# Expert stage: the token vectors of the U dot products are read from PSUM in place of SBUF

## The chip, the cores and the metric

The kernel runs on one core of one Trainium2 chip. The metric is the device time of one execution in microseconds (us). Five engines work side by side, each with its own stream of instructions: TensorE (PE in the profile), VectorE (DVE), ScalarE (ACT), GpSimd (POOL) and SyncE (SP), which only issues transfers here. They wait for one another through semaphores.

## The reference, cut to what matters

Two transformer blocks on 256 tokens of 1024 numbers. The first ends in a layer that retrieves single-neuron experts. That layer is the one that the change touches: `h` is the normed activation, every token picks 16 experts of 16384 in each of 8 heads, so 128 rows of `expert_u` and 128 rows of `expert_v` for each token.

```python
def peer_ffn(h, w_query, sub_keys, expert_u, expert_v):
    q = jnp.einsum('bsd,dk->bsk', h, w_query).reshape(B, S, PEER_HEADS, 2, PEER_HALF)
    sc = jnp.einsum('bshpc,hpnc->bshpn', q, sub_keys)
    s1, i1 = lax.top_k(sc[..., 0, :], 16)
    s2, i2 = lax.top_k(sc[..., 1, :], 16)
    cand_s, cand_i = (16 x 16 sums of s1 and s2), (i1 * 128 + i2)
    top_s, sel = lax.top_k(cand_s, 16)
    idx, gates = cand_i[sel], softmax(top_s)
    # for each chunk of 128 tokens (c), 8 heads (h), 16 experts (k):
    u = expert_u[idx]                                     # (c, h, k, 1024)
    a = gelu(einsum('cd,chkd->chk', h, u)) * gates
    return einsum('chk,chkd->cd', a, expert_v[idx])
```

The first block then adds this to its residual, and the second block (four gated feed-forward layers, an RWKV mixer, a differential attention) follows.

## The kernel before, in words

Up to the expert stage the kernel computes the first block's modulation, projections, attention and the second norm. The normed activation lies feature-major in `hf` (128 partitions of features, 256 tokens in the free dimension), split into two fp32r parts `hh` and `hl` for matmuls.

**Front of the expert stage.** For the first four heads (`EARLY_HEADS`) PE projects the queries (`project`), ACT copies them out of PSUM (`query_out`, L1643), PE multiplies them with the keys (`key_scores`, L1577, banks 2 and 3 in turn) and ACT copies the scores to SBUF (`key_scores_out`, L1649). Beside the first two heads PE also turns `hf` to token-major (`turn_h2`, L1566: eight 128x128 transposes for each half of the tokens, into banks 4 and 5 for tokens 0 to 127 and 6 and 7 for tokens 128 to 255), and ACT copies these banks to `h2tok` in SBUF (`h2_out`, L1636, four copies of 128x512; `h2tok` is a piece of the buffer `aux`). DVE ranks: `rank_experts(u)` finds, for one of the 16 units (two token halves times eight heads), the 16 experts of each of 128 tokens, with max, max-index, replace and 128x256 tensor operations (L1735 to L1787). It writes 16 columns of `expert`, the row numbers.

**The loop.** `STEPS` is 268 steps, one for each of the 256 rows (`NROW`) and `LAG` = 12 more. Row r is one expert for each of 128 tokens: partition p holds the 1024 numbers of the expert of token p. In step i

- POOL issues an indirect DMA that gathers U row i, and one that gathers V row i - 12 (`gather`, L1706). Each moves 128 x 4 KB = 512 KB from HBM. They go to a ring of 12 places (`ring_rows`: 8 in `big`, 2 in `hf`, 2 in `aux`), and POOL waits in `slot_free` until the last user of the place is through with it. The row numbers are read from `expert`, in SBUF.
- DVE waits for U row i to land and forms the 128 dot products (`dot_product`, L1798): a scalar_tensor_tensor over 128x1024 fp32, in0 the row, in1 the tokens' vectors `h2tok[:, r // P, :]`, with a sum to one column of `dots`. Then it does three instructions of the ranking of a unit two ahead, and every eighth step the coefficients (L1809).
- ACT computes gelu of eight dots every eighth step (L1685) and writes diag(coefficient) 128x128 for each V row (L1692), some two steps ahead of its use.
- PE multiplies diag by the V row, two fp32 matmuls of 128x512 (L1616), and accumulates tokens 0 to 127 in banks 4 and 5, and tokens 128 to 255 in banks 6 and 7. Four of the last rows are added by DVE (L1818, L1821).

Heads 4 to 7 have their query projections and key scores inside the first 64 steps, in pieces on PE; `lo.upto` and `hi.upto` (L320 on DVE, L316 on ACT) split weights into high and low parts, a few of them in these steps. Units 0 to 7 rank the first half of the tokens, units 8 to 15 the second. At step 144 DVE adds the first half's result (`add_experts(0)`, L1836 and L1838), and at step 160 POOL issues two small operations (`final_rstd(0)`, L1712 and L1715).

The order on every engine is that of the code; nothing is planned by costs.

Of the kernel before, what the change touches and what calls it, by code (L numbers as in the profile page):

```python
# [17 lines left out]
F32 = mybir.dt.float32  # L18
# [3 lines left out]
ALU = mybir.AluOpType  # L22
# [3 lines left out]
P = 128  # L26
D = 1024
# [60 lines left out]
def build_program(nc, A, out):  # L88
    ctx = ExitStack()
    with ctx:  # L90
# [33 lines left out]
        w_f = sb("w_f", [P, KT, HEADS])  # L124
        bank = [ctx.enter_context(nc.psum_tensor(f"bank{i}", [P, 512], F32)) for i in range(8)]

# [33 lines left out]
        gt1, gt2 = aux[:, 0:D], aux[:, D:2 * D]  # L160
        h2tok = aux[:, 2 * D:4 * D].rearrange("p (a d) -> p a d", a=TT)

# [1394 lines left out]
        def peer_pe(pe):  # L1557
# [3 lines left out]
            def turn_h2(tt):  # L1561
                pe.wait_ge(S("norm_hf"), 8)
                for half in range(2):
                    for j in range(4):
                        k = 4 * half + j
                        mm = pe.transpose(bank[4 + 2 * tt + half][:, j * P:(j + 1) * P],  # L1566
                                          hf[:, k, tt * P:(tt + 1) * P], ident[:, :])
                    mm.then_inc(S("h2tok_tr"), 1)
# [12 lines left out]
            for h in range(EARLY_HEADS):  # L1581
# [3 lines left out]
                key_scores(h)  # L1585
            pe.wait_ge(S("h2tok"), 4)

# [42 lines left out]
        def peer_act(act, hi):  # L1630
            norm_act(act, 1, hi)

            def h2_out(tt):
                for half in range(2):
                    act.wait_ge(S("h2tok_tr"), 2 * tt + half + 1)
                    act.activation(h2tok[:, tt, half * 512:(half + 1) * 512], bank[4 + 2 * tt + half][:, :], ACT.Copy)\  # L1636
                       .then_inc(S("h2tok"), 1)

# [24 lines left out]
            for h in range(EARLY_HEADS):  # L1663
                hi.upto(QRY + h + 2)
                query_out(h)
                key_scores_out(h)
                if h < 2:
                    h2_out(h)
            for i in range(STEPS):
# [6 lines left out]
                if at == 12 and unit < PEER_HEADS - EARLY_HEADS:  # L1676
                    key_scores_out(unit + EARLY_HEADS)
                if i in (0, 13):
                    gate_exp(min(i, 1))
# [111 lines left out]
        def peer_dve(dve, lo, o):  # L1791
            norm_dve(dve, 1, None)

            def dot_product(r):
                turn = u_turn(r)
                row = ring_rows[turn % RROWS]
                row_landed(dve, turn)
                dve.scalar_tensor_tensor(out=row, in0=row, scalar=1.0, in1=h2tok[:, r // P, :], op0=ALU.mult, op1=ALU.mult,  # L1798
                                         accum_out=dots[:, r:r + 1]).then_inc(S("u_used"), 1)
# [67 lines left out]
            lo.upto(QRY + 4)  # L1867
            dve.wait_ge(S("h2tok"), 4)
            ranking = rank_experts(dve, o, 1)
# [1431 lines left out]
```

## Time and profile before

| | |
|---|---|
| median of 3 runs | 2146.63 us |
| lowest and highest | 2139.64 and 2147.71 us |
| the profiled execution's own time | 2155.59 us |
| its span | 2153.8 us |
| granted TensorE clock, mean | 0.977 of full speed |
| busy | PE 1916.3, DVE 1321.4, ACT 806.7, POOL 641.9 us |
| bytes moved by the POOL queue (software_dynamic) | 270.83 MB |
| the gathers (L1706) | first issued at 267.8 us, last at 963.6 us of the span |

The profile is of one execution. Its span is cut in 40 slices for an overview of busy shares; the chain of work that ended last is followed back from the end; groups of instructions are listed with their busy time and the idle time before them. Windows of the trace give the same for a stretch, with the busy share of the 16 DMA engines and the rate that they moved. A row of the timeline has the start in us, the duration in us, engine, line, operation, the written and read names, and in brackets how long the engine sat idle before it and what ended that.

### The profile page before, as it was taken

To read this page: it belongs to the slowest core of one execution; us is meant where nothing else is said; L and a number is where in the kernel's file an instruction comes from. 1 tells how busy PE (TensorE), PEld (TensorE's weight loads), DVE (VectorE), ACT (ScalarE), POOL (GpSimd) and SP (SyncE) were. 2 spreads that over 40 slices of the span, in tenths; PEclk is the share of its full clock that TensorE was granted. 3 is DMA by queue.
4 is the path that set the end of the run, shared out by engine and by line. 5 is a ranking of instruction groups with operands and counts; after the bars stand their busy time and mean duration, and the time that the engine had idled before them with its cause. 6 is when DMAs were issued, how large, how long until landed. Compare 5 with 4: busy or idle time off the path is not lost.

```text
span 2153.8 us, 30579 instructions
## 1 busy us (share of the span) xinstructions
PE 1916.3 (89%) x11797; PEld 1402.5 (65%) x11797; DVE 1321.4 (61%) x2173; ACT 806.7 (37%) x1285; POOL 641.9 (30%) x644
## 2 busy tenths in 40 slices
PE   6999968877777777779999999899999999979999
PEld 4997854422222222227888888888888888868887
DVE  4777686677667656546456765465456545575544
ACT  2335432222111211114445473344443443564443
POOL 1000087777777777762000004340000000000000
PEclk8999989999999999999999999999999999979999
DMA  9982399999999999995554220055554555424553
GB/s 353 321 294 76 118 369 394 402 409 409 409 409 395 383 378 380 380 409 173 194 177 155 98 98 4 27 172 193 180 193 137 175 181 190 146 70 138 193 181 114
DMA packets 255566, 510.35 MB, mean 237 GB/s; under 512 B 14810, under 2 KB 173228, under 8 KB 252380
## 3 DMA queue, kind: packets, MB, share of 16 engines
q1 hardware_dynamic: 177898, 233.95, 32.8%
q0 software_dynamic: 74416, 270.83, 32.2%
q10 hardware_dynamic: 3138, 4.00, 0.6%
q8 instruction: 77, 1.26, 0.2%
q14 instruction: 37, 0.30, 0.0%
HBM read 507.68 MB, written 1.05 MB: 236 GB/s over the span
## 4 chain that ended last, share of the span: by engine, by line
PE 57%; POOL 17%; DMA 10%; issue 7%; DVE 6%; ACT 3%; SPq 0%; DVEq 0%; ACTq 0%
PE bank L640 22%; PE bank L668 11%; POOL big L1706 11%; PE bank L410 10%; DMA big<-in_peer_v,aux 5%; PE bank L1616 3%; POOL aux L1706 3%; POOL hf L1706 3%; DMA hf<-in_peer_v,aux 2%; DMA big<-in_w_mod 2%; PE bank L2413 1%; PE bank L370 1%; PE bank L683 1%; DVE w_lo L320 1%; ACT w_hi L316 1%
## 5 line engine op out<-in xcount | busy, mean ns | idle before, releaser
L320 DVE TENSOR_TENSOR w_lo<-w_raw,w_hi 128x2048 fp32r<-128x2048 f32 x198 | 453.6, 2293 | 271.7 <-ACT w_hi L316 271.5
L316 ACT ACTIVATE w_hi<-w_raw 128x2048 fp32r<-128x2048 f32 x198 | 378.3, 1912 | 229.6 <-PE bank L640 108.0
L1616 PE MATMUL bank<-big 128*128 128x512 f32 x676 | 338.8, 626 | 102.3 <-DMA big<-in_peer_v,aux 100.2
L1616 PEld LDWEIGHTS bank<-big 128*128 128x128 f32 x676 | 117.2, 192 | 309.9 <-DMA big<-in_peer_v,aux 221.4
L1798 DVE SCALAR_TENSOR_TENSOR big<-big,aux 128x1024 f32<-128x1024 f32 x172 | 210.5, 1225 | 148.0 <-DMA big<-in_peer_u,aux 147.7
L640 PE MATMUL bank<-w_hi,hh 128*128 128x512 f32 x704 | 278.9, 396 | 2.8 <-DVE x L1467 1.7
L640 PE MATMUL bank<-w_lo,hh 128*128 128x512 f32 x704 | 274.4, 390 | 0.0
L640 PE MATMUL bank<-w_hi,hl 128*128 128x512 f32 x704 | 265.7, 390 | 0.0
L1706 POOL DMA_INDIRECT big<-in_peer_u,aux x172 | 180.9, 1052 | 76.2 <-issue 52.1
L410 PE MATMUL bank<-hh,w_hi 128*128 128x256 f32 x672 | 194.3, 289 | 3.5 <-DVE w_lo L320 3.1
L1706 POOL DMA_INDIRECT big<-in_peer_v,aux x172 | 181.7, 1056 | 52.4 <-issue 39.0
L410 PE MATMUL bank<-hl,w_hi 128*128 128x256 f32 x672 | 192.4, 286 | 0.0
L410 PE MATMUL bank<-hh,w_lo 128*128 128x256 f32 x672 | 192.3, 286 | 0.0
L930 POOL TENSOR_TENSOR big<-big 128x512 f32<-128x512 f32 x15 | 19.9, 1325 | 474.2 <-ACT big L559 473.8
L640 PEld LDWEIGHTS bank<-w_hi,hh 128*128 128x128 f32 x704 | 132.3, 188 | 29.4 <-issue 3.5
L640 PEld LDWEIGHTS bank<-w_hi,hl 128*128 128x128 f32 x704 | 132.2, 188 | 28.2
L640 PEld LDWEIGHTS bank<-w_lo,hh 128*128 128x128 f32 x704 | 132.4, 188 | 26.2
L1685 ACT ACTIVATE aux<-aux 128x8 f32<-128x8 f32 x32 | 6.7, 208 | 370.4 <-DVE big L1798 253.4
L1692 ACT ACTIVATE big<-ident,aux 128x128 f32<-128x128 f32 x252 | 84.0, 390 | 162.5 <-DVE aux L1809 146.7
L410 PEld LDWEIGHTS bank<-hh,w_hi 128*128 128x128 f32 x672 | 131.3, 195 | 6.4 <-DVE w_lo L320 3.5
L410 PEld LDWEIGHTS bank<-hl,w_hi 128*128 128x128 f32 x672 | 131.4, 195 | 0.1
L410 PEld LDWEIGHTS bank<-hh,w_lo 128*128 128x128 f32 x672 | 131.2, 195 | 0.0
(453 smaller groups left out, 3342.7 us busy)
## 6 DMA issues: line engine op xcount, KB each, us to landing
w_raw<-in_ffn_w_in SPq DMA_DIRECT2D x176, 512.0 KB, 4.6
w_raw<-in_ffn_w_out SPq DMA_DIRECT2D x44, 1024.0 KB, 4.9
big<-in_w_mod SPq DMA_DIRECT2D x24, 1024.0 KB, 7.7
w_raw<-in_w_in SPq DMA_DIRECT2D x22, 1024.0 KB, 9.5
w_raw<-in_rwkv_w_rkv SPq DMA_DIRECT2D x12, 1024.0 KB, 5.2
w_raw<-in_peer_w_query SPq DMA_DIRECT2D x8, 1024.0 KB, 5.6
w_raw<-in_w_kv SPq DMA_DIRECT2D x8, 1024.0 KB, 5.5
w_raw<-in_w_out SPq DMA_DIRECT2D x4, 1024.0 KB, 5.1
```

Of the source, the lines that this page charges most:

```text
L316: act.activation(w_hi[i][:, :], w_raw[i][:, :], ACT.Copy).then_inc(S("w_hi"), 1)
L320: dve.tensor_tensor(w_lo[i][:, :], w_raw[i][:, :], w_hi[i][:, :].bitcast(F32), ALU.subtract)\
L370: return pe.matmul(b[:, part * CW:(part + 1) * CW], lhs, rhs, start=first, stop=last, skip_group_check=True)
L410: mm = pe.matmul(b[:, part * CW:(part + 1) * CW], lhs, rhs, start=(k == 0 and m == 0), stop=(k == KT - 1 and m == 2))
L640: return pe.matmul(bank[b + tt][:, :], a[:, k, tt * P:(tt + 1) * P], w[:, j, :], start=first and half == 0, stop=last and half == 1, skip_ ...
L668: mm = pe.matmul(bank[4 + part][:, :], ap[:, a * T + tt * P:a * T + (tt + 1) * P], wp[:, a, half * 512:(half + 1) * 512], start=(first and ...
L683: mm = pe.transpose(bank[b][:, a * T + tt * P:a * T + (tt + 1) * P], act_f[:, tt, a * P:(a + 1) * P], ident[:, :])
L1616: mm = pe.matmul(bank[4 + 2 * tt + half][:, :], diag[:, r % VDIAGS, :], ring_rows[turn % RROWS][:, half * 512:(half + 1) * 512], start=(r ...
L1692: act.activation(diag[:, r % VDIAGS, :], ident[:, :], ACT.Copy, scale=dots[:, r:r + 1])\
L1706: pool.indirect_dma_start(ring_rows[turn % RROWS], None, table, bass.IndirectOffsetOnAxis(ap=expert[:, r:r + 1], axis=0))\
L1798: dve.scalar_tensor_tensor(out=row, in0=row, scalar=1.0, in1=h2tok[:, r // P, :], op0=ALU.mult, op1=ALU.mult, accum_out=dots[:, r:r + 1]). ...
L2413: mm = pe.matmul(wkv_slot(name, g)[r, col], m[lhs][r, col], m[rhs][r, col], **alone)
```

## The change

PSUM is now declared as four pairs of banks (`bank_pair`), with `bank[i]` a half of a pair. The tokens' vectors that `dot_product` reads are the pairs themselves: pair 3 (banks 6 and 7) for tokens 0 to 127, and pair 1 (banks 2 and 3) for tokens 128 to 255.

- PE transposes the first half of the tokens into banks 6 and 7, and the second half into banks 4 and 5.
- ACT's copies out of PSUM are two in place of four: those of the first half are gone, and those of the second half go to `h2_rest` in SBUF after head 1.
- A new ACT copy, 128x1024 from `h2_rest` to banks 2 and 3 (`h2_second`), stands at step 82, after all key scores have been read.
- DVE waits for the transposes (`h2tok_tr`) before the loop, and at row 128 for `h2_second`. PE waits for the two copies to `h2_rest`.

```diff
-        bank = [ctx.enter_context(nc.psum_tensor(f"bank{i}", [P, 512], F32)) for i in range(8)]
+        bank_pair = [ctx.enter_context(nc.psum_tensor(f"bank_pair{i}", [P, 1024], F32)) for i in range(4)]
+        bank = [bank_pair[i // 2][:, i % 2 * 512:(i % 2 + 1) * 512] for i in range(8)]
...
-        h2tok = aux[:, 2 * D:4 * D].rearrange("p (a d) -> p a d", a=TT)
+        h2tok = [bank_pair[3], bank_pair[1]]
+        h2_rest = aux[:, 2 * D:3 * D]
...
-                        mm = pe.transpose(bank[4 + 2 * tt + half][:, j * P:(j + 1) * P],
+                        mm = pe.transpose(bank[6 - 2 * tt + half][:, j * P:(j + 1) * P],
...
-            pe.wait_ge(S("h2tok"), 4)
+            pe.wait_ge(S("h2_rest"), 2)
...
-            def h2_out(tt):
+            def h2_out():
                 for half in range(2):
-                    act.wait_ge(S("h2tok_tr"), 2 * tt + half + 1)
-                    act.activation(h2tok[:, tt, half * 512:(half + 1) * 512], bank[4 + 2 * tt + half][:, :], ACT.Copy)\
-                       .then_inc(S("h2tok"), 1)
+                    act.wait_ge(S("h2tok_tr"), 3 + half)
+                    act.activation(h2_rest[:, half * 512:(half + 1) * 512], bank[4 + half][:, :], ACT.Copy)\
+                       .then_inc(S("h2_rest"), 1)
+
+            def h2_second():
+                act.wait_ge(S("key_scores_read"), PEER_HEADS)
+                act.wait_ge(S("h2_rest"), 2)
+                act.activation(h2tok[1][:, :], h2_rest, ACT.Copy).then_inc(S("h2_second"), 1)
...
-                if h < 2:
-                    h2_out(h)
+                if h == 1:
+                    h2_out()
...
+                if i == 5 * TOPK + 2:
+                    h2_second()
...
-                dve.scalar_tensor_tensor(out=row, in0=row, scalar=1.0, in1=h2tok[:, r // P, :], op0=ALU.mult, op1=ALU.mult,
+                if r == P:
+                    dve.wait_ge(S("h2_second"), 1)
+                dve.scalar_tensor_tensor(out=row, in0=row, scalar=1.0, in1=h2tok[r // P][:, :], op0=ALU.mult, op1=ALU.mult,
...
-            dve.wait_ge(S("h2tok"), 4)
+            dve.wait_ge(S("h2tok_tr"), 2)
```

The order of PE, DVE, POOL and SP is the same row for row; ACT's changes in two places. First ACT before, at the front of the expert stage (L1643 and L1649 are the query and score copies, L316 a weight split, L1636 the copies of the tokens' vectors):

```order
L316 ACTIVATE w_hi<-w_raw 128x2048
L1643 ACTIVATE big<-bank 128x512
L1649 ACTIVATE big<-bank 128x2x256
L1636 ACTIVATE aux<-bank 128x512 x2
L316 ACTIVATE w_hi<-w_raw 128x2048
L1643 ACTIVATE big<-bank 128x512
L1649 ACTIVATE big<-bank 128x2x256
L1636 ACTIVATE aux<-bank 128x512 x2
L316 ACTIVATE w_hi<-w_raw 128x2048
```

The same place now, with the line numbers of the changed kernel (L318 the split, L1650 and L1656 the query and score copies, L1638 the copies to `h2_rest`):

```order
L318 ACTIVATE w_hi<-w_raw 128x2048
L1650 ACTIVATE big<-bank_pair 128x512
L1656 ACTIVATE big<-bank_pair 128x2x256
L318 ACTIVATE w_hi<-w_raw 128x2048
L1650 ACTIVATE big<-bank_pair 128x512
L1656 ACTIVATE big<-bank_pair 128x2x256
L1638 ACTIVATE aux<-bank_pair 128x512 x2
L318 ACTIVATE w_hi<-w_raw 128x2048
```

The first pair of copies is gone, so the weight split behind it moves up by two instructions. The second place, in the loop at step 82, ACT now (L1694 gelu, L1701 the diagonals, L1644 the new copy):

```order
L1694 ACTIVATE aux<-aux 128x8
L1701 ACTIVATE big<-ident,aux 128x128 x2
L1644 ACTIVATE bank_pair<-aux 128x1024
L1701 ACTIVATE big<-ident,aux 128x128 x6
L1661 ACT_TABLE_LOAD
```

The eight diagonals of one group are now parted by one copy. On DVE the rows stand as they did, with another second input; before, right behind the last instruction of the first ranking:

```order
L1787 TENSOR_TENSOR aux<-w_f 128x16
L320 TENSOR_TENSOR w_lo<-w_raw,w_hi 128x2048 x2
L1798 SCALAR_TENSOR_TENSOR big,aux<-big,aux 128x1024
L1735 MAX aux<-big 128x8 x2
L1739 MAX_INDEX aux<-aux,big 128x8
L1798 SCALAR_TENSOR_TENSOR big,aux<-big,aux 128x1024
```

And now:

```order
L1796 TENSOR_TENSOR aux<-w_f 128x16
L322 TENSOR_TENSOR w_lo<-w_raw,w_hi 128x2048 x2
L1809 SCALAR_TENSOR_TENSOR big,aux<-big,bank_pair 128x1024
L1744 MAX aux<-big 128x8 x2
L1748 MAX_INDEX aux<-aux,big 128x8
L1809 SCALAR_TENSOR_TENSOR big,aux<-big,bank_pair 128x1024
```

Nothing has moved; the dot product reads one SBUF buffer and one pair of banks in place of two SBUF buffers.

## Rows read from the trace of the kernel before

**Rows 1.** Page, chain of work that ended last, by engine and by line:

```profile
PE 57%; POOL 17%; DMA 10%; issue 7%; DVE 6%; ACT 3%; SPq 0%; DVEq 0%; ACTq 0%
PE bank L640 22%; PE bank L668 11%; POOL big L1706 11%; PE bank L410 10%; DMA big<-in_peer_v,aux 5%; PE bank L1616 3%; POOL aux L1706 3%; POOL hf L1706 3%; DMA hf<-in_peer_v,aux 2%; DMA big<-in_w_mod 2%; PE bank L2413 1%; PE bank L370 1%; PE bank L683 1%; DVE w_lo L320 1%; ACT w_hi L316 1%
```

**Rows 2.** Windows: length, busy (x) of PE, PEld, DVE, ACT, POOL; clock, DMA share, GB/s:

```profile
285.00:312.00 27.00, 12.27 (x32) 6.55 (x31) 26.38 (x67) 5.91 (x13) 22.38 (x15) 0.62 1.04 395
312.00:339.00 27.00, 21.16 (x82) 12.06 (x80) 17.63 (x38) 8.71 (x18) 21.56 (x18) 1.00 0.97 358
339.00:420.00 81.00, 69.75 (x227) 35.16 (x226) 59.21 (x144) 20.95 (x46) 63.08 (x59) 1.00 1.02 403
420.00:690.00 270.00, 208.56 (x432) 73.44 (x431) 184.22 (x471) 55.21 (x145) 206.44 (x211) 0.99 1.03 409
690.00:906.00 216.00, 153.77 (x311) 52.41 (x309) 138.49 (x349) 41.92 (x110) 168.30 (x157) 1.00 0.99 378
906.00:933.00 27.00, 22.16 (x43) 7.96 (x44) 12.47 (x21) 2.77 (x9) 20.54 (x22) 0.95 1.03 410
```

**Rows 3.** Line L1706, 420 to 690 us: ns min/median/max; time to landing:

```profile
L1706 POOL DMA_INDIRECT big<-in_peer_v,aux x70: 933/937/1096, 419.9 to 686.0; - x70
...
DMA to landing us min/median/max: 7.7/9.2/10.2
```

**Rows 4.** The same line, 690 to 906 us:

```profile
L1706 POOL DMA_INDIRECT big<-in_peer_v,aux x52: 933/1060/1912, 695.9 to 902.3; - x52
...
DMA to landing us min/median/max: 5.4/6.1/9.0
```

**Rows 5.** Timeline of POOL, 656 to 660 us: two gathers in a row:

```profile
656.77 0.93 POOL L1706 DMA_INDIRECT hf<-in_peer_v,aux  x1 [0.31 <-issue]
658.01 1.94 POOL L1706 DMA_INDIRECT aux<-in_peer_u,aux  x1 [0.30 <-issue]
```

**Rows 6.** Timeline of DVE, the same stretch:

```profile
656.60 1.28 DVE L1836 TENSOR_TENSOR big<-bank,aux 128x512 f32<-128x512 f32 x2
657.91 1.22 DVE L1838 TENSOR_TENSOR x<-x,big 128x1024 f32<-128x1024 f32 x1
```

**Rows 7.** Timeline of POOL, 705 to 712 us:

```profile
705.01 0.94 POOL L1706 DMA_INDIRECT hf<-in_peer_u,aux  x1 [0.30 <-issue]
706.25 1.37 POOL L1706 DMA_INDIRECT hf<-in_peer_v,aux  x1 [0.30 <-issue]
...
709.17 1.58 POOL L1706 DMA_INDIRECT aux<-in_peer_v,aux  x1 [0.30 <-issue]
```

**Rows 8.** Timeline of DVE, the same stretch:

```profile
704.97 0.42 DVE L1781 TENSOR_REDUCE aux<-amask 128x16 f32<-128x256 f32 x1
...
705.59 1.22 DVE L1798 SCALAR_TENSOR_TENSOR big<-big,aux 128x1024 f32<-128x1024 f32 x1
...
708.71 1.23 DVE L1798 SCALAR_TENSOR_TENSOR big<-big,aux 128x1024 f32<-128x1024 f32 x1 [0.74 <-DMA big<-in_peer_u,aux]
```

**Rows 9.** Groups of DVE instructions by line and shape, whole span:

```profile
L1798 DVE SCALAR_TENSOR_TENSOR big<-big,aux 128x1024 f32<-128x1024 f32 x172 | 210.5, 1225 | 148.0 <-DMA big<-in_peer_u,aux 147.7
...
L857 DVE SCALAR_TENSOR_TENSOR big<-bank,small,big 128x256 f32<-128x256 f32 x88 | 38.5, 480 | 87.5 <-ACT big L778 87.5
...
L1775 DVE TENSOR_TENSOR amask<-aux,small 128x256 f32<-128x256 f32 x32 | 13.6, 425 | 1.1
...
L2718 DVE SCALAR_TENSOR_TENSOR hf<-x,vec,big 128x256 f32<-128x256 f32 x8 | 3.4, 480 | 0.0
```

**Rows 10.** Timeline of POOL at the first gather:

```profile
267.79 3.11 POOL L1706 DMA_INDIRECT big<-in_peer_u,aux  x1 [24.03 <-DVE aux L1784]
```

**Rows 11.** Timeline of DVE at the first gather:

```profile
267.48 4.49 DVE L320 TENSOR_TENSOR w_lo<-w_raw,w_hi 128x2048 fp32r<-128x2048 f32 x2
```

**Rows 12.** ACT copies: L1636, and the group nearest to the new one:

```profile
L1636 ACT ACTIVATE aux<-bank x4: 593/600/606, 257.8 to 265.9; 128x512 f32<-128x512 f32 x4
...
L1660 ACT ACTIVATE hh<-x 128x1024 fp32r<-128x1024 f32 x2 | 2.1, 1049 | 13.2 <-DVE x L1838 13.2
```

## The prediction

> **What bounds the kernel now.** I start with the chain of work that ended last [rows 1]. The reader is to see that the indirect gathers stand in it as POOL instructions at L1706 in three names (11, 3 and 3%, together POOL's 17% of the 2153.8 us span) and as transfers of V rows (5 and 2% in the named groups). So while the expert stage runs, some 700 us (the first gather was issued at 267.8 us, the last at 963.6), the pace of the gathers is the pace of the kernel. Everything behind the stage waits for it and shifts with it as a whole.
>
> Next, the windows of the stage [rows 2]. Between 420 and 690 us the 16 DMA engines are busy all the time (share 1.03) and move 409 GB/s; the window at 906 shows 410. No window goes above, so I take 409 to 410 as the ceiling of the transfers. A gather is 0.524 MB, so at the ceiling one passes every 0.524 / 0.409 = 1.28 us and a step of two every 2.56 us. From 690 to 906 the rate is only 378, in 312 to 339 it is 358, in 339 to 420 it is 403, in 285 to 312 it is 395.
>
> Why the rate falls is in line L1706. In the fast stretch the V gathers' median is 937 ns and a gather lands 9.2 us after its issue [rows 3]; with 1.28 us a gather, seven are under way, so there is a queue. In the slow stretch the median of the V gathers in `big` is 1060 ns, up to 1912, and the landing takes 6.1 us, down to 5.4 [rows 4]: the queue has drained, and POOL no longer issues fast enough. Free, POOL needs 0.937 + 0.30 us (the gap before each [rows 5, 7]) = 1.24 us a gather, a little under the 1.28; it has only 0.04 us of slack.
>
> What stretches a gather is seen by laying the two timelines over each other. At 705.01 a gather starts beside a DVE reduction with one input and takes 0.94. At 706.25 one starts inside the dot product that runs from 705.59 to 706.81 and ends at 707.62, 0.81 after it. At 709.17 one starts inside the dot product of 708.71 to 709.94 and ends at 710.75, again 0.81 after it [rows 7, 8]. So a gather needs something near its start that the dot product holds until it ends. It is not DVE as such: at 656.77 a gather runs whole beside L1836, a product of a PSUM bank and an SBUF buffer, in 0.93 us, and the next, at 658.01, starts 0.10 us into L1838, a sum of two SBUF buffers that ends at 659.13, and takes 1.94, to 659.95, 0.82 behind it [rows 5, 6]. That pair is the experiment in small: two SBUF inputs hold the gather, one PSUM and one SBUF input do not.
>
> The Trainium skill, "SBUF — State Buffer", section "Who interferes with whom", says that a DVE instruction with two SBUF inputs contends with a GpSimd instruction that reads SBUF, and one with at most one SBUF input does not. The gather reads its row numbers from SBUF; the pair of rows agrees. The same section infers that a two-input tensor_tensor does not hold descriptor generation, since that writes; by that sentence this change would give nothing. The 1.94 us beside L1838 speak against it.
>
> **The change part by part.** The sum is made against the profiled execution's own 2155.59 us (span 2153.8).
>
> Removed: the hold of 256 dot products on the gathers. In 690 to 906 POOL is busy 168.30 us for 157 instructions; at 0.937 each that would be 147.1, so 21.2 us are stretch [rows 2, 4]. Of this 157 x 0.04 = 6.3 us lay in POOL's slack, and 15 remain. By bytes: 216 x (1 - 378/409) = 16.4 us. I take 16.4. In 312 to 339 it is 27 x (1 - 358/409) = 3.4 us, and there too POOL is busy 21.56 for 18 gathers, 16.9 when free, so it never waits. In 339 to 420 it is 81 x (1 - 403/409) = 1.2 us. In 285 to 312 it would be 0.9, but DVE is busy 26.38 of 27 us there and would not go faster; I count nothing. In 420 to 690 the stretch (206.44 - 211 x 0.937 = 8.7 us) lies beside a full DMA queue and brings nothing. Sum: 21.0 us.
>
> What stays held: the weight splits L320, two SBUF inputs; the first gather takes 3.11 us beside two of them [rows 10, 11], and nothing of that changes. And the ranking's 128x256 operations with two SBUF inputs (L1775 with 425 ns, its neighbours L1758 and L1778 alike, five in a unit of 16 steps) [rows 9]. A gather starts every 1.24 us, so it falls into one of these with 0.425/1.24 = a third, and loses 0.2 us or so: 5 x 0.34 x 0.2 = 0.35 us a unit, against a slack of 32 x 0.04 = 1.3 us. Where every one is caught whole it is 5 x 0.43 = 2.1 a unit, 0.8 above the slack, 14 units: 11 us lost. I take 1 us, near the first.
>
> The dot product itself. The trace shows none with a PSUM input of this size. The nearest rows: L857, with a bank as input, 480 ns for 256 elements; L2718, all SBUF, 480 ns for 256 [rows 9]. So 1225 ns stays. From below it could be 0.08 less (the accumulator's read is apart, and I know no gain); from above, a second pass over the elements, (1225 - 480)/768 x 1024 = 0.99 us more. DVE is busy 138.49 of 216 us with 78 steps, 1.78 a step where 2.56 are to be had [rows 2], so up to 0.78 us more an instruction costs nothing but at the front, where DVE is full for some 12 steps. I take 0.
>
> The Trainium skill, "VectorE: DVE Perf Modes", section on the TRN2 errata, gives a fixed 58 cycles for SBUF sources and 120 for PSUM. By that a dot product would be 62 cycles, as an estimate 0.065 us, longer, and 256 of them 16.5 us if all lay on the path; only the 12 at the front would, under 1 us. The two equal 480 ns rows show no such difference.
>
> ACT: two of four 0.60 us copies at the front are gone [rows 12]. They stood behind the first score copy, which starts the first ranking, so the first gather at 267.79, for which POOL waits on L1784 [rows 10], isn't reached by them. They delayed a weight split for the third head, which DVE takes up only after its first ranking: 0, with 1.2 us as the bound if a split were late for it. The new copy at step 82 is 1.05 us by its nearest row, L1660, with the same shape [rows 12]; ACT is busy 55 of 270 us there, and the diagonals are two steps (5 us) ahead of PE, so it costs 0; queued behind it are six diagonals, and if PE used them at once, 1.05 us. PE's waits: the copies to `h2_rest` are done at the front. DVE's new wait at row 128 is for a copy 46 steps old. PE writes banks 4 and 5 while DVE reads 6 and 7, later 6 and 7 while DVE reads 2 and 3: no bank is shared.
>
> Sum: -21.0 + 1.0 = -20 us, so the profiled execution would come to 2135.6. The median of the runs is 2146.63, 9.0 below the profiled execution. If that is the cost of profiling, the new median is 2146.6 - 20 = 2126.6. If unprofiled executions lost less to the holds (the loss hangs on the phase between POOL and DVE, and 420 to 690 shows a good phase and 690 to 906 a bad one), it is nearer to 2135. I take 2130, between both.
>
> **The rivals.**
>
> A, the forecast: the holds of the dot products go, the DMA engines are the bound at 409 GB/s from 312 us on. 2130, and with its own unknowns 2120 to 2138.
>
> B: the phase shifts so that the ranking's short operations catch the gathers whole. For it: POOL's slack is only 0.04 us a gather. Against: they are 0.43 us long, and 9 us of queue cover them in the mean. 11 of the 20 us are lost: 2138 to 2140.
>
> C: the hold is not one of the port, or does not go with PSUM as second input of this instruction, so that the change doesn't do what it says. For it: only one gather beside L1836 shows PSUM to be free. Against: ends 0.81 to 0.82 us behind each of three holders. The time is 2146.6.
>
> D, on the other side: the dot product from PSUM takes two passes, 1.225 + 0.99 = 2.2 us. A DVE step is then 1.78 + 0.99 = 2.77 us over the 2.56 of the transfers. The loop of 256 steps becomes DVE-bound: 256 x 0.21 = 54 us above the DMA-bound 2130, so 2184. It decides from 0.78 us more an instruction. Against: the equal rows L857 and L2718.
>
> E: 409 GB/s is not the ceiling but POOL's pace locked to DVE. For it: in 420 to 690 U gathers are also stretched a little. Then POOL's free 1.24 us rules, 0.04 us x 512 = 20 us more: 2110. Against: share 1.03, 9.2 us to landing.
>
> **How the numbers follow.** A 0.70, B 0.12, C 0.08, D 0.05, E 0.05. The predicted time is that of A, 2130. The range has A whole, B and the better part of C's side left out only from 2146: 2119 to 2145. About 0.5%, 10.7 us, is what a measurement of this kernel can tell from no change: faster means under 2135.9, slower over 2157.4. A lies under it in nine of ten cases (0.63), E always (0.05), B in a third (0.04): faster 0.72. Same: the rest of A and B and all of C, 0.23. Slower: D, 0.05.
>
> **What would show it.** In the window 690 to 906 (or where these steps then lie) 409 GB/s and a landing time near 9 us say that the bound is the transfers; 378 and 6 us say C. L1706 beside a dot product should stay at 0.94 us, and gathers over 1.2 us should be left only beside L320, L1838 and the ranking's two-input operations; many of 1.2 to 1.4 there say B. The dot product's row should read 1225 ns; 1290 is the page's rule, over 2000 is D. A rate over 415 GB/s says E. The prediction is wrong if the stage from first to last gather (695.8 us now) does not shrink by 15 to 25 us.

## The result, and the profile after

| | before | changed |
|---|---|---|
| median of 20 runs | 2146.66 us | 2141.22 us |
| lowest to highest | 2139.64 to 2159.52 | 2136.74 to 2145.28 |
| ratio to before | | 0.9972 (95%: 0.9960 to 0.9985) |
| profiled execution, span | 2155.59, 2153.8 | 2139.22, 2137.5 |

The change makes the kernel 0.28% faster, 5.4 us in the medians. The forecast was 2130 us, 16.6 under the median then known, from a gain of 20 on the profiled execution. 2141.22 lies inside the stated range of 2119 to 2145, but the gain is a third of the one forecast. The two profiled executions differ by 16.4 us, three times as much as the medians; that gap is the subject of what follows.

The chain of the changed kernel, to be held against [rows 1]: POOL's share has gone from 17% to 7%, the transfers' from 10% to 19%.

```profile
PE 57%; DMA 19%; DVE 8%; POOL 7%; issue 4%; ACT 3%; SPq 0%; DVEq 0%; ACTq 0%; POOLq 0%
```

The windows of the changed kernel, with the columns of [rows 2]:

```profile
285.00:312.00 27.00, 11.87 (x33) 6.43 (x32) 26.38 (x67) 5.91 (x13) 17.80 (x16) 0.68 1.03 397
312.00:339.00 27.00, 23.08 (x83) 12.64 (x83) 19.67 (x42) 9.41 (x20) 20.88 (x21) 1.00 1.03 402
339.00:420.00 81.00, 69.19 (x226) 34.94 (x225) 57.17 (x139) 20.26 (x44) 59.50 (x61) 1.00 1.03 407
420.00:690.00 270.00, 206.29 (x428) 71.72 (x427) 185.61 (x473) 56.09 (x146) 195.90 (x209) 1.00 1.03 409
690.00:906.00 216.00, 165.12 (x334) 56.42 (x333) 144.12 (x358) 43.45 (x116) 156.63 (x167) 1.00 1.03 409
```

378 GB/s has become 409 in 690 to 906, and 358 has become 402 in 312 to 339. POOL's 167 instructions in 690 to 906 take 156.63 us, that is 0.938 each. The gathers' line (L1715 now, min/median/max in ns) in that stretch, against [rows 4]:

```profile
L1715 POOL DMA_INDIRECT big<-in_peer_v,aux x56: 932/936/1022, 689.6 to 904.8; - x56
...
DMA to landing us min/median/max: 11.2/13.1/14.4
```

The median is 936 ns in place of 1060, the largest 1022 in place of 1912, and the queue, 6.1 us to landing before, is now 13.1. Taken over all gathers of this window, whatever they write: before, 78 of them start inside a dot product and 49 of these take more than 1.0 us, with a median end 0.81 us behind the dot product; now 79 start inside one, and the longest takes 0.945 us. POOL now waits 20.7 us of this window for PE to give a place of the ring back. The groups of the dot product and of the new ACT copy:

```profile
L1809 DVE SCALAR_TENSOR_TENSOR big<-big,bank_pair 128x1024 f32<-128x1024 f32 x172 | 209.7, 1220 | 140.5 <-DMA big<-in_peer_u,aux 139.8
```

```profile
L1644 ACT ACTIVATE bank_pair<-aux x1: 1006/1006/1006, 485.3 to 485.3; 128x1024 f32<-128x1024 f32 x1
```

From PSUM the dot product takes 1220 ns where it took 1225 [rows 9], and nobody waited for the new copy.

To compare executions I take three numbers from each trace: when the first gather was issued, when the last addition of expert rows (`add_experts(1)`, L1838 and L1849 after) started, and the span. "Stage" below is the second minus the first, and "behind the stage" is the span from the second number on.

| execution | first gather | stage | behind the stage |
|---|---|---|---|
| before, profile of the prediction | 267.8 | 709.1 | 1176.9 |
| changed | 267.4 | 694.0 | 1176.1 |

### The profile page after: what moved, and what is told of

The parts are those of the page before. It is cut to its first block, busy times and chain, and to the rows that moved or that the text cites. A ratio compares the mean times of both kernels' runs of the same rounds, so it can differ in the third digit from the quotient of the medians.

```text
span 2137.5 us, 30580 instructions
## 1 busy us (share of the span) xinstructions
PE 1910.9 (89%) x11797; PEld 1398.2 (65%) x11797; DVE 1320.6 (62%) x2173; ACT 806.9 (38%) x1284; POOL 593.9 (28%) x644
## 4 chain that ended last, share of the span: by engine, by line
PE 57%; DMA 19%; DVE 8%; POOL 7%; issue 4%; ACT 3%; SPq 0%; DVEq 0%; ACTq 0%; POOLq 0%
PE bank_pair L642 23%; PE bank_pair L670 11%; PE bank_pair L412 10%; DMA aux<-in_peer_v,aux 7%; DMA big<-in_peer_v,aux 6%; POOL big L1715 4%; PE bank_pair L1618 3%; DMA hf<-in_peer_v,aux 2%; DMA big<-in_w_mod 2%; DMA big<-in_peer_u,aux 2%; PE bank_pair L2424 1%; POOL hf L1715 1%; PE bank_pair L372 1%; POOL aux L1715 1%; DVE w_lo L322 1%
## 5 line engine op out<-in xcount | busy, mean ns | idle before, releaser
L318 ACT ACTIVATE w_hi<-w_raw 128x2048 fp32r<-128x2048 f32 x198 | 378.4, 1912 | 231.1 <-PE bank_pair L642 107.4
L1618 PE MATMUL bank_pair<-big 128*128 128x512 f32 x676 | 335.8, 621 | 95.6 <-DMA big<-in_peer_v,aux 93.6
L1809 DVE SCALAR_TENSOR_TENSOR big<-big,bank_pair 128x1024 f32<-128x1024 f32 x172 | 209.7, 1220 | 140.5 <-DMA big<-in_peer_u,aux 139.8
L642 PE MATMUL bank_pair<-w_hi,hh 128*128 128x512 f32 x704 | 278.6, 396 | 2.8 <-DVE x L1469 1.7
L642 PE MATMUL bank_pair<-w_lo,hh 128*128 128x512 f32 x704 | 274.2, 389 | 0.0
L642 PE MATMUL bank_pair<-w_hi,hl 128*128 128x512 f32 x704 | 265.5, 390 | 0.0
L412 PE MATMUL bank_pair<-hh,w_hi 128*128 128x256 f32 x672 | 193.4, 288 | 3.9 <-DVE w_lo L322 3.2
L412 PE MATMUL bank_pair<-hl,w_hi 128*128 128x256 f32 x672 | 191.8, 285 | 0.0
L412 PE MATMUL bank_pair<-hh,w_lo 128*128 128x256 f32 x672 | 191.7, 285 | 0.0
L1715 POOL DMA_INDIRECT big<-in_peer_u,aux x172 | 169.5, 986 | 79.5 <-issue 48.5
L1715 POOL DMA_INDIRECT big<-in_peer_v,aux x172 | 163.5, 951 | 66.4 <-PE bank_pair L1618 36.0
L642 PEld LDWEIGHTS bank_pair<-w_hi,hh 128*128 128x128 f32 x704 | 132.2, 188 | 29.4 <-issue 3.5
L642 PEld LDWEIGHTS bank_pair<-w_lo,hh 128*128 128x128 f32 x704 | 132.4, 188 | 26.3
L1701 ACT ACTIVATE big<-ident,aux 128x128 f32<-128x128 f32 x252 | 83.9, 390 | 157.1 <-DVE aux L1820 142.4
L1694 ACT ACTIVATE aux<-aux 128x8 f32<-128x8 f32 x32 | 6.7, 208 | 358.9 <-DVE big L1809 249.8
```

What stands on the lines that cost most here:

```text
L318: act.activation(w_hi[i][:, :], w_raw[i][:, :], ACT.Copy).then_inc(S("w_hi"), 1)
L412: mm = pe.matmul(b[:, part * CW:(part + 1) * CW], lhs, rhs, start=(k == 0 and m == 0), stop=(k == KT - 1 and m == 2))
L642: return pe.matmul(bank[b + tt][:, :], a[:, k, tt * P:(tt + 1) * P], w[:, j, :], start=first and half == 0, stop=last and half == 1, skip_ ...
L1618: mm = pe.matmul(bank[4 + 2 * tt + half][:, :], diag[:, r % VDIAGS, :], ring_rows[turn % RROWS][:, half * 512:(half + 1) * 512], start=(r ...
L1701: act.activation(diag[:, r % VDIAGS, :], ident[:, :], ACT.Copy, scale=dots[:, r:r + 1])\
L1715: pool.indirect_dma_start(ring_rows[turn % RROWS], None, table, bass.IndirectOffsetOnAxis(ap=expert[:, r:r + 1], axis=0))\
```

## The experiments

The runs fell on chips of two kinds. On some the windows reach 409 GB/s as in the two profiles above; on others they stay near 370 in the middle of the stage for every version, and each version takes some 50 to 60 us longer. Times are only compared with runs of before on the same chip.

### Both kernels again, unchanged

No edit. Seven further profiled executions of before and two of the changed kernel (its series after_rounds stands further down).

> The kernel before, unchanged, another execution. Theory 'phase' (the loss to the holds differs from execution to execution, and the profile of before that the prediction was read from had a bad one): the stage's windows differ from those read before; the time of the execution follows them: an execution of 2146 us shows a loss of some 9 us less in 690 to 906 us, that is a mean of 395 GB/s or so in place of 378, and a time to landing nearer to 9 us. Rival 'profiling costs 9 us' (the holds are alike in all executions): the window 690 to 906 shows 378 GB/s again and the profiled execution 2155 us. Rival 'lost elsewhere': the window is alike and the difference of times lies outside the stage.

> The kernel before, unchanged, a second time. Phase: again another distribution of the loss over the stage; last gather issued anywhere from 950 to 964 us, and the spread of the executions (20 us over 20 runs of before) is the spread of that number. Profiling cost: 963 us again, 378 GB/s again.

> The kernel before, unchanged, a third time. As for the second: phase says that span and the time of the last gather move together, one for one, with different losses at different places; the rivals say that the stage is the same each time.

> The changed kernel, unchanged, another execution. Phase: without the holds nothing hangs on it, so 409 GB/s in every window from 339 to 933 us again, landing 13 us, last gather issued at 944 us within 2 us; executions of 2145 us are then late for a cause outside the stage (its 20 runs go from 2136.7 to 2145.3). Rival 'the stage varies with the change too': a window under 405 GB/s or a last gather 4 us or more off.

> The kernel before, unchanged, to be read beside the next runs of the same chip. Theory 'phase and supply': the time of the last gather is the sum of two things, the rate at which this chip's memory delivers (409 GB/s in the two first profiles, 370 in the last four) and the holds, which cost only what goes beyond POOL's slack at that rate. Where the rate is 409 the loss to the holds lies between 5 and 25 us and differs from the 22.8 us of the first profile; where it is 370 it is 10 to 16 us. Rival 'the same loss always': last gather at 963 to 964 us where the rate is 409.

> The changed kernel, unchanged, beside the run of before. Theory: gathers of 0.937 us and never a window under the chip's rate by more than 1%, whatever the rate; last gather at 944 us at 409 GB/s. Rival: the stage of the changed kernel varies as that of before does.

> The kernel before, a further look. Theory 'phase': stage of 695 to 705 us in the common case where the memory gives 409 GB/s, that is a loss of 2 to 10 us to the holds against the changed kernel; the 709 us of the first profile is at the edge. Rival: 707 us or more again.

> The kernel before, unchanged. Theory 'phase': where the memory gives 409 GB/s, the stage takes 696 to 703 us, so 2 to 9 us over the changed kernel's 694; the loss is at other places than in the earlier profiles. Rival: 707 us or more. Where it gives 370 GB/s, 750 to 757 us as in four earlier looks.

> As before_again_6, another execution: the same range, another distribution of the losses over the windows.

| execution | us | first gather | stage | behind it | GB/s in 690 to 906 |
|---|---|---|---|---|---|
| before_again_4 | 2147.30 | 270.0 | 696.4 | 1179.1 | 400 |
| before_again_6 | 2157.94 | 269.0 | 707.5 | 1179.7 | 382 |
| before_again_7 | 2142.34 | 267.7 | 696.9 | 1176.0 | 401 |
| after_again_2 | 2145.83 | 270.4 | 693.9 | 1179.8 | 409 |
| before_again_1, slow memory | 2204.93 | 268.4 | 757.1 | 1177.7 | 361 |
| before_again_2, slow memory | 2197.53 | 268.2 | 750.8 | 1176.8 | 366 |
| before_again_3, slow memory | 2204.34 | 267.5 | 754.6 | 1180.5 | 363 |
| before_again_5, slow memory | 2204.79 | 268.1 | 757.0 | 1177.9 | 364 |
| after_again, slow memory | 2189.28 | 270.1 | 742.8 | 1174.6 | 371 |

The rivals "profiling costs 9 us" and "the same loss always" fall: with full-rate memory the stage of before took 709.1, 707.5, 696.9 and 696.4 us, that of the changed kernel 694.0 and 693.9. So before has a bad course, 14 us over the changed kernel, and a good one, 3 us over it. The profile of the prediction had the bad one. The windows of before_again_7, the good course:

```profile
312.00:339.00 27.00, 20.40 (x73) 11.61 (x72) 17.56 (x38) 7.83 (x16) 21.52 (x18) 0.91 0.95 348
...
420.00:690.00 270.00, 208.28 (x437) 72.91 (x435) 185.30 (x472) 55.18 (x145) 206.10 (x212) 1.00 1.03 409
690.00:744.00 54.00, 39.14 (x80) 13.54 (x80) 39.63 (x108) 10.12 (x29) 41.95 (x40) 1.00 0.98 378
744.00:906.00 162.00, 123.81 (x250) 42.00 (x249) 103.78 (x251) 32.59 (x85) 123.58 (x127) 1.00 1.03 409
```

And those of before_again_6, the bad one:

```profile
312.00:339.00 27.00, 21.81 (x84) 12.53 (x82) 18.89 (x42) 8.71 (x18) 22.11 (x17) 1.00 0.99 369
...
420.00:690.00 270.00, 208.48 (x435) 73.60 (x434) 184.98 (x470) 55.30 (x145) 206.63 (x209) 0.99 1.02 407
690.00:744.00 54.00, 39.33 (x81) 13.38 (x80) 39.48 (x108) 9.10 (x25) 42.09 (x42) 1.00 0.99 382
744.00:906.00 162.00, 115.44 (x233) 39.64 (x234) 99.45 (x244) 32.81 (x85) 126.05 (x119) 1.00 1.00 382
```

Both fall to about 380 at 690 us. One is back at 409 after 54 us, the other stays at 382 to 906 and is at 409 only in 906 to 933. So of the four profiles at full-rate memory two lose 162 x (1 - 382/409) = 10.7 us or more in the second part of the window (12.7 with the 377 GB/s of the first profile), and two next to nothing. The gathers show the same: in 54 us of a slow stretch all gathers together are stretched by 4.4 to 5.8 us over 0.937 us each, in 54 us at 409 GB/s by 1.4 to 2.8 us. before_again_6 misses its expectation of 696 to 703 us with 707.5, which is what the rival said. I had also expected the loss to wander; in fact it stands at the same two places each time, 312 to 339 and from 690 on, and mainly its length differs. What ends the slow stretch after 54 us in one execution and lets it go on in another is not shown.

Two more expectations missed. before_again_4 was to lose 5 to 25 us to the holds; its stage is 2.5 us over the changed one (by its windows 7.4, see the last part). And the first three executions of before fell on slow memory, where the rates expected can't be judged; that span and last gather move one for one doesn't hold there: from before_again_2 to before_again_3 the last gather moves by 2.1 us (1009.1 to 1011.2) and the span by 6.8, 3.7 of it behind the stage.

How often the bad course comes can be estimated. Outside the stage the eight executions that were profiled at 409 GB/s, with the two such of the next two experiments, take 1443.4 to 1450.2 us; with a stage of 707.5 to 709.1 that makes an execution of 2153 us or more. 3 of the 20 runs of before in the result are that long, and 2 of the 23 beside before_again_4. By this estimate the bad course is the rare one, though two of the four profiles have it.

The last expectation of after_again also holds, in after_again_2, where the memory allows the comparison: the changed kernel's own spread comes from outside the stage. Its two executions at full-rate memory differ by 6.6 us, 3.0 of it before the first gather (267.4, 270.4) and 3.7 behind the stage (1176.1, 1179.8). Before has the same spread there.

### The two small POOL operations moved

```diff
-                if i == V0_DONE + 20:
+                if i == NROW - 12:
                     final_rstd(0)
```

> Kernel before, with final_rstd(0), the two small POOL operations at step 160, moved to step 244. In the profile that the prediction was read from, the rate fell from 409 to 378 GB/s at 690 us, where they stand. Theory 'phase': they shift POOL against DVE, and the dot products begin to catch the V gathers from there; moved to step 244, the rate stays near the ceiling to the end in an execution where it had been there at 690, and the median falls by 0 to 8 us against before (less where the phase falls into the bad state by itself). Rival 'the second half has another cause' (the ranking of the second half, the banks): the rate still falls at 690 us and the time is the same within 2 us.

2145.78 us median against 2147.35, ratio 1.0002 (0.9983 to 1.0021): no change. Its profile has a stage of 701.0 us with 406 GB/s in 420 to 690 and 398 in 690 to 906. The fall no longer begins at 690, where the rate is 407 and 406 GB/s for 20 us, but it comes: after a dip to 367 in 670 to 680 it is 372 and 367 in 717 to 744 and 744 to 771, and then 409 to 410 to the end. The theory's fall of the median did not come; the time is as the rival said. So these operations are not the cause of the loss; whether they set the moment at which it begins can't be told from one profile. The hope that moving them cures the second half is wrong.

### One half of the rows back to SBUF

```diff
-...in1=h2tok[r // P][:, :], op0
+...in1=h2tok[0][:, :] if r < P else h2_rest, op0        # after_second_sbuf
+...in1=h2_first if r < P else h2tok[1][:, :], op0       # after_first_sbuf, with two ACT copies to h2_first, for which DVE waits ahead of the loop
```

> Changed kernel, with the dot products of rows 128 to 255 reading the SBUF copy h2_rest in place of the banks; all else as changed. Theory 'hold': gathers beside them end 0.81 us behind the dot product again, in the second half alone; the first half stays at 0.937 us. The queue stands full when the second half begins (13 us to landing), so the loss is smaller than in before: 0 to 12 us against the changed kernel, with the time to landing falling from 13 to 9 us or less. Rival 'front' (the gain is made in the first windows, by ACT's copies): no change of time and of gathers in the second half.

> Changed kernel, with the dot products of rows 0 to 127 reading an SBUF copy (two ACT copies of 128x512 are back) and those of rows 128 to 255 the banks. The counterpart of after_second_sbuf, which took 693.1 us from the first gather to the last addition of expert rows, as the changed kernel (694.0 and 693.9), where before took 709.1 and 696.4. Theory 'fill early' (the holds cost where the queue is short, above all at 285 to 339 us, and nothing once a full queue of 13 us covers them): holds and a queue of 8 to 9 us in the first half, 358 to 365 GB/s in 312 to 339 us, no holds in the second half, and there a landing time that rises; 695 to 700 us for the stage, that is 2 to 5 us over the changed kernel. Rival 'second half' (the holds of the second half are the gain): the stage as in the changed kernel, 694.

> The changed kernel with the first half's vectors in SBUF, beside the changed kernel. Theory 'fill early': slower than the changed kernel by 1 to 4 us, stage 695 to 698 us where the memory gives 409 GB/s, since the queue is short in the front and the holds fall there. Rival 'second half': as the changed kernel within 1 us.

> The changed kernel, as the measure for the next two on the same chip. Theory ('queue full early, slowest transfer engine bounds'): ratio to before 0.995 to 0.998; where the memory delivers 409 GB/s the stage takes 693 to 695 us with a trickle of some 25 GB/s for 4 to 6 us at the end of the gathers.

after_second_sbuf: 2142.04 us, 0.9967 of before (0.9952 to 0.9982), as good as the changed kernel. Stage 693.1 us. The holds are there again, and the queue pays for them (gathers, 690 to 906 us):

```profile
L1715 POOL DMA_INDIRECT big<-in_peer_v,aux x56: 933/1010/1905, 690.8 to 905.5; - x56
...
DMA to landing us min/median/max: 7.7/7.9/9.2
```

It enters the second half with 13.0 us to landing and comes down to 7.9, with 405 GB/s in this window. Before enters with 9.2 and comes down to 6.1 in its bad course. 54 of the gathers of this window are held over 1.0 us, where before had 49 in the bad course, and the time is none the worse. So with a queue that is full at the start of the second half, its holds cost nothing that can be measured, and once the first half is free, freeing the second adds nothing.

The counterpart ran on chips with slow memory only. after_first_sbuf gave 0.9969 (0.9956 to 0.9982) with a stage of 754.3 us. after_first_sbuf_2 can be set beside the changed kernel (after_rounds) on the same chip:

| | median us | ratio to before | stage | GB/s in 312 to 339 |
|---|---|---|---|---|
| after_rounds | 2194.49 | 0.9953 (0.9934 to 0.9972) | 745.4 | 399 |
| after_first_sbuf_2 | 2197.72 | 0.9971 (0.9957 to 0.9985) | 750.5 | 365 |

The rate in 312 to 339 us falls back as the theory said (356 in after_first_sbuf; before has 350 to 369). Both ratios share the same runs of before; set against each other, the 6 and 12 runs differ by 3.2 us in the medians and 4.1 in the means (95%: some 1.5 to 6.7). So the holds of the first half do cost something on this chip, as "fill early" expects, but not the whole gain of 10.1 us. What the second half's holds cost there, and what the first half's cost at 409 GB/s, was not run, and the expected stages of 695 to 700 us and times to landing can't be judged on these chips. That the first half matters more is therefore not shown.

### The port by itself

One product of 128x512 more on DVE in steps 130 to 239; its result is used by nobody.

```diff
+                if P + 2 <= i < NROW - 16:
+                    o.wait()
+                    o(dve.tensor_tensor(extra, h2_rest[:, 0:512], extra_in, ALU.mult))   # after_extra_sbuf
+                    o(dve.tensor_tensor(extra, bank[2][:, :], extra_in, ALU.mult))       # after_extra_psum
```

> Changed kernel, with one more product of 128x512 in each of the steps 130 to 239 on DVE, from two SBUF buffers (0.69 us each; its result is used by nobody). Theory 'hold by two SBUF inputs': gathers that start beside it are stretched by up to 0.56 us, many of them over 1.0 us in the second half, and the landing time falls from 13 us to 10 or less; time +0 to +12 us. Rival 'the DVE load alone': the same as after_extra_psum in gathers and time.

> The same extra product, with its first input from PSUM bank 2 in place of SBUF: 0.69 us again, so DVE is loaded alike. Theory: no gather is stretched by it, median and nearly all at 0.937 us, landing 13 us in the second half; time as that of the changed kernel, or the little that DVE's load adds. Rival: as after_extra_sbuf.

DVE's extra instruction is 688 ns from SBUF and 686 from PSUM. The gathers (L1716 here) beside the SBUF form, timeline of POOL and then of DVE:

```profile
703.56 1.44 POOL L1716 DMA_INDIRECT big<-in_peer_v,aux  x1 [0.30 <-issue]
705.31 1.44 POOL L1716 DMA_INDIRECT hf<-in_peer_u,aux  x1 [0.30 <-issue]
707.05 1.44 POOL L1716 DMA_INDIRECT hf<-in_peer_v,aux  x1 [0.30 <-issue]
```

```profile
703.50 0.69 DVE L1890 TENSOR_TENSOR aux<-aux 128x512 f32<-128x512 f32 x1
...
705.24 0.69 DVE L1890 TENSOR_TENSOR aux<-aux 128x512 f32<-128x512 f32 x1
...
706.99 0.69 DVE L1890 TENSOR_TENSOR aux<-aux 128x512 f32<-128x512 f32 x1
```

Each gather ends 0.81 us behind the product (704.19 to 705.00), as in [rows 5 to 8]. In the PSUM form of the same stretch the third gather below starts inside the product, at 706.45, and takes 0.94:

```profile
703.96 0.94 POOL L1716 DMA_INDIRECT aux<-in_peer_u,aux  x1 [0.30 <-issue]
705.20 0.94 POOL L1716 DMA_INDIRECT aux<-in_peer_v,aux  x1 [0.30 <-issue]
706.45 0.94 POOL L1716 DMA_INDIRECT big<-in_peer_u,aux  x1 [0.30 <-issue]
```

```profile
704.19 0.69 DVE L1890 TENSOR_TENSOR aux<-bank_pair,aux 128x512 f32<-128x512 f32 x1
...
705.93 0.69 DVE L1890 TENSOR_TENSOR aux<-bank_pair,aux 128x512 f32<-128x512 f32 x1
```

Over 690 to 906 us, 38 gathers start inside the SBUF form, 28 of them take more than 1.0 us, up to 1.44; 48 start inside the PSUM form, and the longest of these takes 0.941. Of all gathers of the PSUM run in this window none is longer than 1.06. POOL was busy 153.16 us for 152 instructions with the SBUF form and 139.52 for 149 with the PSUM form. So the hold is shown to belong to the second SBUF input and not to DVE's load. The times, 0.9952 (0.9929 to 0.9975) and 0.9963 (0.9949 to 0.9978), are alike, and the profiled stage is 753.4 us for both, so here more holds cost no time, which was the low end of what I expected. POOL's slack on that chip may be why (at 370 GB/s a gather passes every 1.42 us in place of 1.28), but that is argued and not shown: on the chip of after_rounds, with memory as slow, taking the dot products' holds away gained 10.1 us. The expected fall of the time to landing can't be read from these two traces, and the changed kernel without the addition did not run on this chip.

### The weight splits behind a part of the ranking

```diff
-            lo.upto(QRY + 4)
             dve.wait_ge(S("h2tok_tr"), 2)
             ranking = rank_experts(dve, o, 1)
+            for _ in range(13):
+                next(ranking, None)
+            lo.upto(QRY + 4)
```

> Changed kernel, with the two weight splits (two SBUF inputs, 4.49 us together) that follow the first ranking put behind thirteen instructions of the second ranking, mostly with one input. Theory: the first gather takes 0.94 in place of 3.11 us and the next 0.94 in place of 1.60, the first U row lands 2 to 3 us sooner, and the transfers, which bound the stage, start that much sooner: stage 1 to 3 us shorter, 691 to 693 us. Rival: the splits hold two later gathers as much, or DVE, full at 285 to 312 us, becomes late: no change or up to 2 us longer.

> The late splits, beside the changed kernel. Theory: 1 to 6 us faster than the changed kernel (0.9919 of before on the last chip, where the changed kernel with additions had 0.995 to 0.997), from the front of the stage: the first gathers unheld, the queue full sooner. Rival: no difference beyond 1 us, the last chip's ratio was that chip's slow memory.

0.9919 of before (0.9903 to 0.9935) and 0.9924 (0.9905 to 0.9943). In the second series, beside the changed kernel, its six runs lie from 2184.32 to 2190.84 us, those of the changed kernel from 2190.20 to 2195.97; the medians, 2187.20 and 2194.49, differ by 7.3 us, more than the 1 to 6 expected. The first gathers, to be held against [rows 10], and the splits:

```profile
268.84 1.26 POOL L1715 DMA_INDIRECT big<-in_peer_u,aux  x1 [24.98 <-DVE aux L1793]
270.40 0.96 POOL L1715 DMA_INDIRECT big<-in_peer_u,aux  x1 [0.30 <-issue]
271.67 1.11 POOL L1715 DMA_INDIRECT big<-in_peer_u,aux  x1 [0.30 <-issue]
273.08 2.44 POOL L1715 DMA_INDIRECT big<-in_peer_u,aux  x1 [0.30 <-issue]
```

```profile
272.43 4.47 DVE L322 TENSOR_TENSOR w_lo<-w_raw,w_hi 128x2048 fp32r<-128x2048 f32 x2
```

The first gather is nearly unheld, and the hold falls on the fourth, when three rows are under way. The profiled stages of the two series are 746.8 and 742.0 us, that of the changed kernel beside the second 745.4. The profiled executions, too, happen to differ by 7.3 us: 1.5 ahead of the first gather, 3.4 in the stage and 2.4 behind it. 3.4 us is no more than the changed kernel's own difference on such chips (742.8 in after_again, 745.4 here), and in 312 to 339 us the rate is 400 GB/s against 399, so the queue is not seen to fill better. The gain is measured twice; that it comes from the front of the stage is not shown. It has the lowest ratio of all versions that ran, on chips with slow memory both times; on a chip with 409 GB/s it was not tried.

## Why the prediction was wrong

Points that held, each with its number. The dot product's hold on the gathers is one of two SBUF inputs and is gone with a PSUM input (extra pair; 936 ns). The dot product costs nothing more from PSUM (1220 ns, where 1225 was expected, 1290 was one rival and over 2000 another). The ceiling is the transfers' 409 to 410 GB/s with a full queue, so E is out: POOL has slack and waits 20.7 us for PE in 690 to 906, and the rate is the same 409. The windows that were to recover did: 402, 407, 409 GB/s. ACT's edits and the new waits cost nothing that shows. B did not come, C and D neither. Even the sign that the prediction set itself was met in the profiled pair: from the first to the last gather it was 695.8 us and is 676.8, 19.0 less. In the two good executions of before it is 684.2 and 683.5, so against them it shrinks by 7 us only.

What failed is the size, in two terms of the sum.

**The 16.4 us of 690 to 906 was one execution's.** The step "216 x (1 - 378/409) = 16.4 us. I take 16.4" takes the loss of one profile as that of the kernel. By the same formula the good executions lose 4.8 and 4.2 us in this window (400 and 401 GB/s). Four profiles of before show 14 to 15 us over the changed stage twice and 3 us twice. The prediction saw the sign of it: the profiled execution stood 9.0 us above the median, and it named a good and a bad phase. It then took 2130 "between both". Of the 20 runs of before, whose median is 2146.66, three are of the length of the bad course, and the two bad profiles, 2155.59 and 2157.94 us, lie at the upper end of the 2139.64 to 2159.52; the two good ones have 2147.30 and 2142.34. Subtracting the bad course's 20 us from the median counted a loss that the median did not hold. That the one profile read was of the rare course was bad luck; the price of it was in the step. Profiling itself costs nothing that can be seen: the changed kernel's profiled execution, 2139.22, is under its median.

**Even in its own execution 20 us became 15.1.** The step that failed here is the one that turns the mean rate into time, "By bytes": it takes the stage to end when the bytes are through at 409 GB/s. The stage went from 709.1 to 694.0. By bytes the whole gain is there: the windows of [rows 2] against those of the changed kernel give 20.2 us, and the full rate ends at about 971 us before and 949 after. But a row has landed only when its last part has, and the parts don't end together. Windows of 2 us at the end of the gathers, before (from 968) and changed (from 948):

```profile
968.00:970.00 2.00, 1.51 (x4) 0.38 (x2) 1.21 (x1) 0.00 (x0) 0.00 (x0) 1.00 1.01 404
970.00:972.00 2.00, 1.91 (x5) 0.96 (x6) 1.93 (x3) 0.00 (x0) 0.00 (x0) 1.00 0.40 160
972.00:974.00 2.00, 2.00 (x6) 0.86 (x5) 0.59 (x1) 0.00 (x0) 0.00 (x0) 1.00 0.00 0
```

```profile
948.00:950.00 2.00, 1.54 (x4) 0.49 (x3) 1.28 (x1) 0.54 (x2) 0.00 (x0) 1.00 0.66 268
950.00:952.00 2.00, 1.51 (x4) 0.38 (x2) 1.25 (x1) 0.00 (x0) 0.00 (x0) 1.00 0.13 51
952.00:954.00 2.00, 1.98 (x4) 0.68 (x4) 0.80 (x2) 0.00 (x0) 0.00 (x0) 1.00 0.06 25
954.00:956.00 2.00, 1.49 (x4) 0.77 (x5) 1.93 (x3) 0.00 (x0) 0.00 (x0) 1.00 0.10 35
```

Before, the transfers stop at once. Changed, a trickle of 25 to 51 GB/s at a DMA share of 0.06 to 0.13 goes on for 6 us; a share of 0.06 is one engine of 16 (409/16 = 25.6). The packets in the trace bear this out: from 951.0 to 956.5 us 35 packets of 4096 bytes stand one behind the other, each 0.159 us long and starting 0.155 us after the last, with nothing of the gathers beside them. That is the work of a single engine, some 5.5 us behind the rest. PE starts its last three rows at 954.5, on a V row that lands out of this trickle, where it started them at 970.1 before: 15.6 us sooner, not 22. after_again_2 has the same trickle (27, 25, 18 GB/s from 954 to 960), again 35 packets. In the five profiles of before at 409 GB/s the last such row of packets is of five or fewer. The mean rate of 16 engines is no bound of a transfer that needs all of them. Why this engine is behind, and when in the stage it falls back, is not shown.

The two terms together fit the good executions as well: by their windows they lose 8.4 us (before_again_7) and 7.4 us (before_again_4) against the changed kernel, and their stages are 3 us longer, so there too some 5 us of the bytes' gain are lost at the end.

So 20 us were 15 in that execution and about 3 in the good ones; the medians say 5.4. The range's lower side, too, was drawn around 20 us in every execution, and the chance of "same" (0.23) stood for B, C and the upper end of A, none of it for either of these two terms.

## What to carry to other kernels

A term read from a profile whose time stands off the median by half the expected gain is a term of that execution. Look first at whether the loss is steady in the trace (one window at 409 and the next at 378 with the same instructions is not), and price it from the median's side. A hold on the engine that issues transfers may cost nothing while the queue is long (after_second_sbuf, from 13 us down to 7.9). Where the queue fills, ahead of the loop's steady state, is then the first place to look; at 409 GB/s this was not tried. Where a transfer is spread over many engines, ask when the last of them is through, and not only what they move together. And keep a DVE instruction with two SBUF inputs away from gathers that GpSimd issues, or give it one input from PSUM.

## What the runs showed of the hardware that I had not expected

The same kernels ran at 409 GB/s in the middle of the stage on some chips and at 360 to 375 on others, with a stage of 694 and of 743 to 745 us for the changed kernel; the part behind the stage did not differ (1174.6 to 1181.5 us in all profiles). One of the 16 transfer engines worked on alone for 5.5 us at the end of the gathers with a time to landing of 13.1 us there, for 2.3 us with one of 9.2 (after_second_sbuf, 15 packets), and for under 1 us in the profiles of before at 409 GB/s, with 7.9 to 9.2 us. And the same kernel of before, with the same order on every engine, took a stage of 696.4 and 696.9 us in two executions and of 707.5 and 709.1 in two others.
